# RWKV chunk inverse: the transposed half of each step on the other half of the partitions, and its two updates issued in turn

## The reference, cut to what matters

```python
def rwkv7_step(state, inp):
    r_t, w_t, k_t, v_t, a_t, b_t = inp
    sa = jnp.einsum('bhvk,bhk->bhv', state, a_t)
    state = (state * w_t[:, :, None, :] + sa[..., None] * b_t[:, :, None, :]
             + v_t[..., None] * k_t[:, :, None, :])
    return state, jnp.einsum('bhvk,bhk->bhv', state, r_t)
...
    seqs = (tm(r_h), tm(w_h), tm(k_h), tm(v_h), tm(-kk), tm(kk * a_h))
    _, y = lax.scan(rwkv7_step, jnp.zeros((B, H, N, N), f32), seqs)
```

## Time and profile before

| | us |
|---|---|
| median of three runs | 3031.8 |
| lowest, highest | 3029.65, 3033.29 |
| the profiled execution, its own time | 3032.06 |
| its span, first to last instruction | 3030.6 |
| of it, the scores of group 1 to the end of group 2 | about 914 to 1117 |

### The profile page before, as it was taken

One profiled execution on the slowest core, in us unless ns is written; L12 is line 12 of the kernel. 1 busy time (PEld: TensorE's weight loads), 2 busy tenths in 40 slices (PEclk: granted clock), 3 DMA queues, 4 the chain that ended last, 5 costly groups with the idle time before them and its releaser, 6 DMA issues.

```text
span 3030.6 us, 51902 instructions
## 1 busy us (share of the span) xinstructions
PE 2792.0 (92%) x22106; PEld 2657.9 (88%) x22106; DVE 2037.2 (67%) x2757; ACT 1561.6 (52%) x2170; POOL 183.8 (6%) x223
## 2 busy tenths in 40 slices
PE   7998899999899889996899777999999999999996
PEld 7997799999788789995899766899999999999996
DVE  5666665665552436557555574788889898888994
ACT  4445444544221214442444423676777777776773
POOL 1000000000003305001310010000000000000000
PEclk9998999999995669998899887999999999999999
DMA  5542245455230004541355322789889898998991
GB/s 218 194 168 98 98 163 185 145 189 188 97 137 16 2 29 181 184 174 70 112 181 182 133 75 100 276 332 337 333 307 346 324 345 326 344 332 310 343 365 49
DMA packets 84043, 605.43 MB, mean 200 GB/s; under 512 B 9320, under 2 KB 9448, under 8 KB 11168
## 3 DMA queue, kind: packets, MB, share of 16 engines
q1 hardware_dynamic: 81872, 594.05, 53.9%
q10 hardware_dynamic: 1584, 4.85, 0.4%
q0 software_dynamic: 352, 3.15, 0.3%
HBM read 600.96 MB, written 1.05 MB: 199 GB/s over the span
## 4 chain that ended last, share of the span: by engine, by line
PE 86%; DVE 10%; ACT 3%; issue 1%; DMA 0%; ACTq 0%; DVEq 0%
PE bank L389 84%; DVE arena L1838 3%; DVE weights_lo L379 1%; PE bank L2182 1%; ACT weights_hi L371 1%; DVE rstd L436 0%; DVE source_lo_scratch L1279 0%; ACT x_T L485 0%; DVE source_lo L407 0%; PE bank L1461 0%; PE bank L778 0%; DMA x_T<-in_x 0%; DVE arena L957 0%; DVE normed_T L443 0%; DVE arena L977 0%
## 5 line engine op out<-in xcount | busy, mean ns | idle before, releaser
L379 DVE TENSOR_TENSOR weights_lo<-raw_weights,weights_hi 128x1024 fp32r<-128x1024 f32 x820 | 995.5, 1226 | 480.8 <-ACT weights_hi L371 469.3
L371 ACT CAST weights_hi<-raw_weights 128x1024 fp32r<-128x1024 f32 x820 | 852.5, 1048 | 527.0 <-PE bank L389 482.4
L389 PE MATMUL bank<-source_hi,weights_hi 128*128 128x256 f32 x2400 | 692.7, 289 | 63.7 <-DVE weights_lo L379 23.5
L389 PE MATMUL bank<-source_lo,weights_hi 128*128 128x256 f32 x2400 | 687.7, 287 | 0.0
L389 PE MATMUL bank<-source_hi,weights_lo 128*128 128x256 f32 x2400 | 687.4, 286 | 0.0
L389 PE MATMUL bank<-weights_hi,source_hi 128*128 128x256 f32 x1856 | 535.9, 289 | 0.0
L389 PEld LDWEIGHTS bank<-source_hi,weights_hi 128*128 128x128 f32 x2400 | 470.0, 196 | 68.9 <-issue 44.4
L389 PE MATMUL bank<-weights_lo,source_hi 128*128 128x256 f32 x1856 | 524.7, 283 | 0.0
L389 PE MATMUL bank<-weights_hi,source_lo 128*128 128x256 f32 x1856 | 524.3, 283 | 0.0
L389 PEld LDWEIGHTS bank<-source_lo,weights_hi 128*128 128x128 f32 x2400 | 470.1, 196 | 0.8 <-issue 0.7
L389 PEld LDWEIGHTS bank<-source_hi,weights_lo 128*128 128x128 f32 x2400 | 469.6, 196 | 0.0
(11 more groups left out here) (350 smaller groups left out, 3435.0 us busy)
## 6 DMA issues: line engine op xcount, KB each, us to landing
raw_weights<-in_exp_w SPq DMA_DIRECT2D x201, 1024.0 KB, 5.1
arena<-in_exp_w SPq DMA_DIRECT2D x135, 1024.0 KB, 5.0
raw_weights<-in_ffn_w_gate SPq DMA_DIRECT2D x44, 1024.0 KB, 4.9
raw_weights<-in_ffn_w_up SPq DMA_DIRECT2D x44, 1024.0 KB, 5.0
raw_weights<-in_ffn_w_down SPq DMA_DIRECT2D x44, 1024.0 KB, 4.8
raw_weights<-in_dense_w SPq DMA_DIRECT2D x33, 1024.0 KB, 4.8
raw_weights<-in_attn_w_in SPq DMA_DIRECT2D x12, 1024.0 KB, 4.8
raw_weights<-in_w_in SPq DMA_DIRECT2D x12, 1024.0 KB, 4.8
```

The source lines that it names most:

```text
L371: k.act.copy(k.weights(j)[0], raw_half(k, j)).then_inc(k.w_hi_ready, 1)
L379: k.dve.tensor_tensor(lo, raw_half(k, j), hi.bitcast(F32), ALU.subtract).then_inc(k.w_ready, 1)
L389: return k.pe.matmul(dst, lhsT, rhs, start=start, stop=stop, skip_group_check=shared)
```

## The change

The transposed inverse, `X` and the right-hand side `Xs` of chunk parity c move to the other half of the partitions, `part(1 - c)`. The x step's products thereby go from `part(c)` to `part(1 - c)`, the update of `TiT` stays within a half, and the update of `Ti` goes from one half to the other. The two updates of a t step are issued in turn, matrix by matrix, and no longer one after the other; the update of `Ti` lands in `b0`, in the place of `X`, and no longer in `b1`. `Xs`, `BH` and `KH` go to `b1`, behind the x steps of levels 1, 2 and 3, and ACT copies them there, ahead of the t step. POOL no longer makes `TiT`: TensorE computes `MabT` a second time with the halves exchanged (8 more products in ab), and DVE masks it and adds the identity (4 products of mask and score and 2 additions a pair, where there were 2 and 1).

```diff
-            ins = mm(k, mat(z.b[h], c, s), z.ar[part(h), 0, chunk_columns(s, c)], z.bt[part(h), chunk_columns(s, c)],
-                     True, True)
+            mm(k, mat(z.b[h], c, s), z.ar[part(h), 0, chunk_columns(s, c)], z.bt[part(h), chunk_columns(s, c)],
+               True, True)
+    for s in range(TT):
+        for h, c in QUADRANTS:
+            ins = mm(k, mat(z.b[h], 1 - c, 2 + s), z.bt[part(h), chunk_columns(s, c)],
+                     z.ar[part(h), 0, chunk_columns(s, c)], True, True)
     ins.then_inc(*p.step((kt, "ab")))
...
-        if 0 < li < 4:
-            pe.wait_ge(*a.at((kt, ("Xs", "BH", "KH")[li - 1])))
         lev, X = z.lev[li % 2], z.X[li]
         for m in range(N_MAT):
             for c in range(2):
-                ins = mm(k, dense(b0[part(c), m * C // 2:(m + 1) * C // 2], size), mat(lev, c, m),
+                ins = mm(k, dense(b0[part(1 - c), m * C // 2:(m + 1) * C // 2], size), mat(lev, c, m),
                          half_columns(mat(z.Ti, c, m), size, 0), True, True)
         ins.then_inc(*p.step((kt, "x", li)))
+        if li == 1:
+            for m in range(N_MAT):
+                for c in range(2):
+                    ins = mm(k, mat(b1, 1 - c, m), z.MakT[part(c), m // 2 + m % 2 * 2, :], mat(z.VN, c, m), True, True)
+            ins.then_inc(*p.step((kt, "Xs")))
+        elif 1 < li < 4:
+            dst, src = (("BH", z.bt), ("KH", z.kt_))[li - 2]
+            pe.wait_ge(*g.at((kt, dst)))
+            for s in range(TT):
+                ins = pe.transpose(b1[:, s * P:(s + 1) * P], src[:, s * P:(s + 1) * P], ident)
+            ins.then_inc(*p.step((kt, dst)))
         yield
         pe.wait_ge(*a.at((kt, "X", li)))
         if li == 0:
-            pe.wait_ge(*g.at((kt, "TiT")))
+            pe.wait_ge(*d.at((kt, "TiT")))
+        elif li < 4:
+            pe.wait_ge(*a.at((kt, ("Xs", "BH", "KH")[li - 1])))
         for m in range(N_MAT):
             for c in range(2):
                 ins = mm(k, dense(b1[part(c), m * C // 2:(m + 1) * C // 2], size), mat(X, c, m),
                          half_columns(mat(z.TiT, c, m), size, 1), True, True)
-        if not last:
-            at = N_MAT * C // 2
-            for m in range(N_MAT):
+            if not last:
                 for c in range(2):
-                    ins = mm(k, dense(b1[part(c), at + m * C // 2:at + (m + 1) * C // 2], size), mat(z.TiT, c, m),
+                    ins = mm(k, dense(b0[part(1 - c), m * C // 2:(m + 1) * C // 2], size), mat(z.TiT, c, m),
                              half_columns(mat(X, c, m), size, 0), True, True)
...
+            for to, at, mask in ((z.Ti, 0, 8), (z.TiT, P, 2)):
+                dve.tensor_tensor(mats(to)[:, 2 * h:2 * h + 2, :], z.b[h][:, at:at + P].rearrange("p (m t) -> p m t", m=2),
+                              z.mask(mask)[:, 0:2, :], ALU.mult).then_inc(*d.step((kt, "T0", h, mask)))
+    dve.wait_ge(*d.at((kt, "T0", 1, 2)))
     dve.tensor_tensor(mats(z.Ti), mats(z.Ti), z.mask(9), ALU.add).then_inc(*d.step((kt, "t", -1)))
+    dve.tensor_tensor(mats(z.TiT), mats(z.TiT), z.mask(9), ALU.add).then_inc(*d.step((kt, "TiT")))
...
-    pool.tensor_tensor(mats(z.TiT), z.MabT, z.mask(2), ALU.mult).then_inc(*g.step((kt, "TiT0")))
-    pool.wait_ge(*g.at((kt, "TiT0")))
-    pool.tensor_tensor(mats(z.TiT), mats(z.TiT), z.mask(9), ALU.add).then_inc(*g.step((kt, "TiT")))
```

More of the change, by code:

```diff
@@ L1468, in pair_tensor @@
             for h in range(2):
-                ins = mm(k, z.b[h][part(c), P:P + HEAD], z.ar[part(h), 0, chunk_columns(s, c)], z.S[n][part(h), :],
+                ins = mm(k, z.b[h][part(1 - c), P:P + HEAD], z.ar[part(h), 0, chunk_columns(s, c)], z.S[n][part(h), :],
                          True, True)
@@ L1476, in pair_tensor @@
         for h in range(2):
-            ins = mm(k, b1[part(c), h * HEAD:(h + 1) * HEAD], mat(z.TiT, c, 2 * h + s), mat(z.Xs, c, 2 * s + h),
+            ins = mm(k, b1[part(c), h * HEAD:(h + 1) * HEAD], mat(z.TiT, 1 - c, 2 * h + s), mat(z.Xs, 1 - c, 2 * s + h),
                      True, True)
@@ L1521, in pair_scalar @@
         act.copy(half_columns(z.X[li], size, 0), dense(b0[:, 0:N_MAT * C // 2], size)).then_inc(*a.step((kt, "X", li)))
+        if 0 < li < 4:
+            name, dst = (("Xs", z.Xs), ("BH", z.BH), ("KH", z.KH))[li - 1]
+            act.wait_ge(*p.at((kt, name)))
+            act.copy(dst, b1[:, 0:T]).then_inc(*a.step((kt, name)))
         yield
-        if li < 3:
-            name, dst = (("Xs", z.Xs), ("BH", z.BH), ("KH", z.KH))[li]
-            act.wait_ge(*p.at((kt, name)))
-            act.copy(dst, b0[:, 0:T]).then_inc(*a.step((kt, name)))
         yield
@@ L1568, in pair_vector @@
     for h in range(2):
-        dve.tensor_tensor(mats(z.Ti)[:, 2 * h:2 * h + 2, :], z.b[h][:, 0:P].rearrange("p (m t) -> p m t", m=2),
-                          z.mask(8)[:, 0:2, :], ALU.mult).then_inc(*d.step((kt, "Ti0", h)))
-    dve.wait_ge(*d.at((kt, "Ti0", 1)))
+        for to, at, mask in ((z.Ti, 0, 8), (z.TiT, P, 2)):
+            dve.tensor_tensor(mats(to)[:, 2 * h:2 * h + 2, :], z.b[h][:, at:at + P].rearrange("p (m t) -> p m t", m=2),
+                              z.mask(mask)[:, 0:2, :], ALU.mult).then_inc(*d.step((kt, "T0", h, mask)))
+    dve.wait_ge(*d.at((kt, "T0", 1, 2)))
     dve.tensor_tensor(mats(z.Ti), mats(z.Ti), z.mask(9), ALU.add).then_inc(*d.step((kt, "t", -1)))
+    dve.tensor_tensor(mats(z.TiT), mats(z.TiT), z.mask(9), ALU.add).then_inc(*d.step((kt, "TiT")))
     yield
@@ L1579, in pair_vector @@
         if li == 0:
-            dve.wait_ge(*g.at((kt, "TiT")))
+            dve.wait_ge(*d.at((kt, "TiT")))
         piece = half_columns(z.TiT, size, 1)
@@ L1584, in pair_vector @@
             piece = half_columns(z.Ti, size, 0)
-            dve.tensor_tensor(piece, piece, dense(b1[:, N_MAT * C // 2:N_MAT * C], size), ALU.add)\
+            dve.tensor_tensor(piece, piece, dense(b0[:, 0:N_MAT * C // 2], size), ALU.add)\
                 .then_inc(*d.step((kt, "t", li)))
@@ L1594, in pair_vector @@
             for h in range(2):
-                piece = mat(z.Xs, c, 2 * s + h)
-                ins = dve.tensor_tensor(piece, z.b[h][part(c), P:P + HEAD], piece, ALU.add)
+                piece = mat(z.Xs, 1 - c, 2 * s + h)
+                ins = dve.tensor_tensor(piece, z.b[h][part(1 - c), P:P + HEAD], piece, ALU.add)
             ins.then_inc(*d.step((kt, "Xs", n)))
```

1 line of the change is left out of this document (removed).

## The result

| | before | after |
|---|---|---|
| median of four runs, us | 3032.14 | 2981.41 |
| lowest, highest | 3029.65, 3033.29 | 2975.13, 2988.67 |
| profiled execution, its span | 3032.06, 3030.6 | 2975.13, 2973.7 |

The ratio is 0.9835, with a 95% interval of 0.9805 to 0.9864.

The account below looks back on a forecast made before the run. PE's pace in the levels at clock 0.50, and ahead of it DVE's in the start of the inverse, bound the kernel; 27.2 saved less 5.4 lost, 21.8 us off 3031.8, gives 3010 us, range 2985 to 3022 (8 in 10).

Parts of the forecast that it names:

- The t step: Levels of both groups: 32 instructions round four quadrants take 0.85 us a pair instead of 1.70, at clock 0.50.
- no gain from four quadrants: Rival, t steps: four quadrants go no faster than two, t steps stay at 1.70 us; 3037 us, chance 0.08.
- What it is worth: Levels of both groups: 32 t steps save 0.85 us each, 27.2 us in all, 20 us as the lower end.
- The moved products: Levels: products and transposes moved from behind t steps to behind x steps are the same number and cost nothing.
- the clock rival: Levels: the clock rises above 0.50; 2968 us, or 2980 to 3000 if late or in one group; chance 0.13.
- Both quadrants of a row half start together: Levels, argument against a clock rise: so the rows are not fed for more of the time than now.
- `Xs` at level 0 did not raise it: Level 0, argument against a clock rise: today's denser Xs products there did not raise the clock.
- its late half: Levels: the clock rises late or in one group, giving 2980 to 3000 us; taken into the forecast's range.
- The start of the inverse: DVE ahead of the levels: 1.64 us a pair instead of 0.87, 5.4 us lost over two groups, ends 3.3 and 7.
- The 0.66 of the earlier trace: Start of the inverse: first pair's addition took 0.66 instead of 0.44 us beside POOL's masks, which may come again.
- The order of waits: Levels: 2.6 us of cover hides ACT's and DVE's answers; rival that they come late gives 3020 us, chance 0.04.

Follow-up runs that it names:

- e2: Kernel before with only Xs, BH and KH moved behind the x steps of levels 1, 2 and 3, into b1; 2982.97 us, ratio 0.9843.
- e9: Kernel before with both the moved Xs, BH, KH and the changed start of the inverse, still two quadrants; 2992.99 us, ratio 0.9892.
- e7: Changed kernel with BH, KH and Xs behind the x steps of levels 1, 2 and 3, so Xs at level 3; 2992.41 us, ratio 0.9882.
- e3: Kernel before with only the changed start of the inverse, in the old halves; 3040.23 us, ratio 1.0028.
- e5: e2 with Xs behind the x steps of level 0, BH and KH staying at levels 2 and 3; 3000.73 us, ratio 0.9896.
- after_again: The changed kernel itself, unaltered, run four more times against the kernel before; 2979.57 us, ratio 0.9847.
- e10: Changed kernel with POOL's scaling for BH and KH held back until DVE has finished the start of the inverse; 2980.33 us, ratio 0.9845.
- e1: Changed kernel with the update of Ti issued behind that of TiT again, not in turn; 2976.05 us, ratio 0.9822.
- e4: e2 with each t product but the last level's issued a second time into a free quadrant, result unread; 3026.27 us, ratio 0.9981.
- e8: e2 with two already met waits put ahead of each t product; 3037.55 us, ratio 1.0024.

## Why the prediction was wrong, step by step

**The t step: right.** 0.85 us at clock 0.50, to the digit. Neither rule that spoke against it is seen here. "TensorEngine Tiling (Array Packing)", Performance Considerations, of the Trainium skill has an overhead of some 60 cycles a matmul; the trace has 26.6 ns a matmul over four quadrants (0.85 us for 32), 32 cycles at 1.2 GHz. Gotcha 1 of the same page of the Trainium skill says that different row tiles can't access one PSUM bank at the same time; here both row halves write to `b0` and to `b1` within one step, and a matmul takes no longer than the 30 ns or so of the ab products in the earlier trace rows, of 64 columns, whose row halves write to separate banks. The rival "no gain from four quadrants" is out at either clock (2.06 against 3.71 us a round at the upper one).

**What it is worth: wrong.** 32 t steps at the lower clock were to save 27.2 us, but only the first round of each group runs at that clock, 8 steps and 6.8 us. At the upper clock two quadrants need half the time already: a round of four t steps takes 3.71 us in e2 and 2.06 in the changed kernel. An estimate from these: two rounds at 3.4 us saved and six at 1.65 make 16.7, and the four holes take back 3.3. What was measured is the 13 us between e9 and after, and in these is also what the clock's earlier rise in group 1 brings.

**The moved products: the step that failed.** The prediction said that the products and transposes moved to behind the x steps "are the same number", and left it there. As work that is true; each takes what it took. But e2 shows that this move alone brings 48 us: once the wider `Xs` products stand among the shorter x steps, the clock rises there, for all that follows in the group. So the step that failed is that these edits "cost nothing" and change nothing: they were put at 0, and they measured -48 us. An edit with no cost of its own changed the pace of the rest of each group.

**The case against the clock rival: wrong in both points.** "Both quadrants of a row half start together": in the timeline of the changed kernel the two column halves of a row half start some 30 and 70 ns apart, in turn. "`Xs` at level 0 did not raise it": true of its place behind a t step of 1.70 us, and no evidence for any other place. The rival itself was sized well, 2968 us, with 2980 to 3000 for a late rise. It had half of the cause: it looked to the t steps, which e7 shows to raise the clock in one group and not in the other, and not to `Xs`, which do it without them. With 0.13 for it and only its late half in the range, the range ended at 2985, 4 us too high.

**The start of the inverse: right in kind, too small.** 9.1 us (e3), 9.5 by the rows, for 5.4. The term had 1.64 us a pair; the rows have 2.5, 2.3, 2.2. The additions take 0.61 to 0.94 and not 0.44. The 0.66 of the earlier trace rows was mentioned and not used.

**The order of waits: right.** Once the start of the inverse is done, TensorE waits for no other engine in the levels of the changed kernel, even at the upper clock. In e5 it does, for POOL.

**The sum as it is.** -48 for the moved products, +9 for the start, -13 for the four quadrants: -52, measured -51. The -13 is the difference that was left between e9 and the changed kernel, so only the start, 9 alone and 10 on top of e2, tests that the parts add. In the traces the changed kernel leaves group 2 61 us earlier (1117.2 and 1055.9 us), and its span is 57 shorter: 4 us are lost far behind, at the start of the experts. The chain there, before:

```profile
1899.91 3.68 PE bank L2216 x16
```

And after:

```profile
1837.79 0.90 PE bank L2216 x3
1838.69 2.38 issue
1841.07 3.14 PE bank L2216 x13
```

A second hole without a releaser, within the transposes, costs most of it, 6.42 us for the 16 instead of 3.68, and the 32 matmuls behind (from 1904.30 and 1844.91 us) take 6.17 us instead of 3.81: their clock is 0.59, where it was 1.00. No experiment bears on it, so why the hole is there stays open. So does the spread of the changed kernel, 2975 to 2989 us: the mean clock of its four runs goes from 0.949 (slowest) to 0.957 and the traces of `after_again` and e10 show a group that fell back, but what decides it from run to run wasn't found.

## What to carry to other kernels

When a stretch runs at the lower clock with TensorE busy throughout, ask of each reordering what then stands side by side: here wider products beside the shortest narrow ones raised the clock for everything behind, and the same products behind longer steps didn't. Once the clock is up, look again at who was just in time at half pace, here POOL's masks and, it seems, the supply of instructions. And try each part of a change alone, the harmless ones too: the part costed at nothing was the gain, and the issue in turn, which the title names, was nothing.

## What the hardware showed that I had not expected

- Quadrants advance by themselves: a product in a free quadrant starts ahead of an earlier one in a busy quadrant (927.41 against 927.51 and later), so that the order of issue within 16 products didn't matter (e1).
- Small float32 products in four quadrants at the upper clock come in pieces: 127 matmuls in 2.2 us, then a hole of 1.3 to 1.5 us in which TensorE waits for nothing that the profile shows (e4), 36 a us over all. That it is out of instructions then is argued from the size of the pieces.
- The same program text gave clock 1.00 in one group and 0.50 in the other (e7), and two short waits of TensorE at the upper clock, 1.2 us together, were followed by 52 us at 0.50 (e5).
- Two waits that are already met ahead of each product cost more than half of TensorE's pace in the t steps at the upper clock: 1.17 us for 8 products against 0.47 (e8, e2).
